# A decoder layer on one core: scores issued ahead of the state-space stages, S5 result and GELU by halves, and two moves before the MLP

## The reference, cut to what matters

```python
proj = _modulate(_rmsnorm(h, norm_mix), sh1, sc1) @ w_in           # u, q, k, v, qi, ki, wi
y = S5(u)                                                          # 32 groups x 64 states
y = jax.nn.gelu(y); y_ssm = y * jax.nn.sigmoid(y @ w_glu + b_glu)
s_idx = sum_h(relu(qi_h @ ki) * wi_h); sel = top_k(s_idx, 128)     # causal
p = softmax(where(selected, q @ k / 8, -inf)); y_attn = p @ v      # 8 heads
h = h + g1 * (concat(_rmsnorm(y_ssm), _rmsnorm(y_attn)) @ w_out)
up = _causal_dwconv(_modulate(_rmsnorm(h, norm_ffn), sh2, sc2) @ w_up, conv_w, conv_b)
h = h + g2 * ((jax.nn.gelu(gate) * val) @ w_down)
```

## Time and profile before

| | |
|---|---|
| median of 3 runs | 800.43 us (797.33 to 802.19) |
| profiled execution | 801.28 us |
| its span | 799.5 us |
| mean granted TensorE clock | 0.951 |
| busy: TensorE, VectorE, ScalarE, GpSimd | 89%, 61%, 41%, 32% |

### The profile page before, as it was taken

One profiled execution on the slowest core, in us unless ns is written; L12 is line 12 of the kernel. 1 busy time (PEld: TensorE's weight loads), 2 busy tenths in 40 slices (PEclk: granted clock), 3 DMA queues, 4 the chain that ended last, 5 costly groups with the idle time before them and its releaser, 6 DMA issues.

```text
span 799.5 us, 9833 instructions
## 1 busy us (share of the span) xinstructions
PE 709.3 (89%) x3524; PEld 565.6 (71%) x3524; DVE 488.4 (61%) x872; ACT 328.2 (41%) x476; POOL 257.6 (32%) x204
## 2 busy tenths in 40 slices
PE   0689999998668858889949999999999999999998
PEld 0667876776555635668849788888887887888886
DVE  2989588997599977868852576566545554100005
ACT  4246345346321452523246544544555555210110
POOL 1006697308501300000220444334442444334440
PEclk9999999999588869999979999999999999999999
DMA  9932131260033583753370322333223222332212
GB/s 338 341 109 80 53 106 53 79 184 1 1 45 46 106 315 109 264 211 106 105 260 31 106 69 89 105 105 105 70 88 105 97 67 99 106 105 101 64 46 106
DMA packets 65608, 91.46 MB, mean 114 GB/s; under 512 B 11914, under 2 KB 39330, under 8 KB 65443
## 3 DMA queue, kind: packets, MB, share of 16 engines
q1 hardware_dynamic: 60800, 84.72, 33.7%
q10 hardware_dynamic: 4771, 6.26, 2.3%
HBM read 86.28 MB, written 4.69 MB: 114 GB/s over the span
## 4 chain that ended last, share of the span: by engine, by line
PE 72%; DVE 17%; ACT 4%; issue 3%; DMA 3%; ACTq 1%; SPq 0%; DVEq 0%
PE bank L1544 21%; PE bank L1546 20%; PE bank L1545 20%; PE bank L1549 3%; DVE arena L1102 2%; PE bank L1857 2%; PE bank L1770 1%; PE bank L1750 1%; DVE w_lo L1096 1%; DMA y_dram<-xh 1%; DVE arena L1248 1%; DMA xh<-in_x 1%; DVE stat L1049 1%; DVE stat L1245 1%; PE bank L1880 1%
## 5 line engine op out<-in xcount | busy, mean ns | idle before, releaser
L466 POOL TENSOR_TENSOR w_lo<-w_raw,w_hi 128x2048 fp32r<-128x2048 f32 x35 | 161.5, 4614 | 408.0 <-ACT w_hi L658 199.4
L1544 PE MATMUL bank<-act_hi,w_hi 128*128 128x512 f32 (+2 forms) x384 | 148.5, 387 | 9.9 <-DVE act_lo L1480 8.4
L1545 PE MATMUL bank<-act_lo,w_hi 128*128 128x512 f32 (+2 forms) x384 | 147.4, 384 | 0.0
L1546 PE MATMUL bank<-act_hi,w_lo 128*128 128x512 f32 (+2 forms) x384 | 147.3, 384 | 0.0
L1544 PE MATMUL bank<-w_hi,act_hi 128*128 128x512 f32 x240 | 100.7, 420 | 5.8 <-DVE act_lo L1137 4.2
L1546 PE MATMUL bank<-w_hi,act_lo 128*128 128x512 f32 x240 | 96.8, 403 | 0.0
L1545 PE MATMUL bank<-w_lo,act_hi 128*128 128x512 f32 x240 | 96.7, 403 | 0.0
L1544 PEld LDWEIGHTS bank<-act_hi,w_hi 128*128 128x128 f32 x384 | 73.4, 191 | 25.2 <-issue 9.0
L658 ACT ACTIVATE w_hi<-w_raw 128x2048 fp32r<-128x2048 f32 x26 | 49.8, 1914 | 100.4 <-PE bank L1546 85.8
L1545 PEld LDWEIGHTS bank<-act_lo,w_hi 128*128 128x128 f32 x384 | 73.3, 191 | 14.7 <-issue 0.2
L1546 PEld LDWEIGHTS bank<-act_hi,w_lo 128*128 128x128 f32 x384 | 73.3, 191 | 14.6
(11 more groups left out here) (296 smaller groups left out, 1180.5 us busy)
## 6 DMA issues: line engine op xcount, KB each, us to landing
w_raw<-in_w_up SPq DMA_DIRECT2D x44, 512.0 KB, 4.4
w_raw<-in_w_down SPq DMA_DIRECT2D x22, 512.0 KB, 4.2
w_raw<-in_w_in SPq DMA_DIRECT2D x10, 1024.0 KB, 5.1
arena<-in_w_ada SPq DMA_DIRECT2D x4, 2048.0 KB, 18.6
arena<-in_w_ada SPq DMA_DIRECT2D x8, 1024.0 KB, 8.3
xh<-in_x SPq DMA_DIRECT2D x8, 512.0 KB, 8.0
w_raw<-in_w_out SPq DMA_DIRECT2D x4, 1024.0 KB, 12.9
s_mem<-in_w_ada SPq DMA_DIRECT2D x4, 1024.0 KB, 8.5
```

What stands on the lines that cost most here:

```text
L466: nc.gpsimd.tensor_tensor(w_lo[:, slot, 0:width], w_raw[:, slot, 0:width], w_hi[:, slot, 0:width].bitcast(F32), ALU.subtract).then_inc(S[" ...
L1544: T.matmul(dst, lhs_hi, rhs_hi, start=start, stop=False)
L1545: T.matmul(dst, lhs_hi, rhs_lo, start=False, stop=False)
L1546: return T.matmul(dst, lhs_lo, rhs_hi, start=False, stop=stop)
```

## The change

Four edits. In TensorE's list the S5 stages of a unit come one pass later, after the scores of the next pair and directly ahead of the unit's own probabilities. The store and load of y and the GELU are done by halves of the channels, at units 20 and 23, and the gate stages of S5 move: `g` of the first half from unit 22 to 21, the four `glu` from 25 to 28 to 26 to 29, with the squares of y accordingly. The loads of the second gate leave ScalarE's queue and stand in SP's, behind the first two units of the MLP. The low part of `U_UP` is VectorE's instead of GpSimd's.

```diff
-         15: ("y", 0, 0), 18: ("y", 1, 0), 22: ("g", 0, 0), 24: ("g", 1, 0),
-         25: ("glu", 0, 0), 26: ("glu", 1, 0), 27: ("glu", 2, 0), 28: ("glu", 3, 0)}
+         15: ("y", 0, 0), 18: ("y", 1, 0), 21: ("g", 0, 0), 24: ("g", 1, 0),
+         26: ("glu", 0, 0), 27: ("glu", 1, 0), 28: ("glu", 2, 0), 29: ("glu", 3, 0)}
+GELU_AT = {20: 0, 23: 1}
-SQUARE_AT = {19: (0,), 20: (1,), 28: (2, 4), 29: (5,), 30: (6,), 31: (7,)}
+SQUARE_AT = {19: (0,), 20: (1,), 28: (2,), 29: (4,), 30: (5,), 31: (6, 7)}
@@ SP
+            def y_load(half):
+                ns = slice(256 * half, 256 * half + 256)
+                sp.wait_ge(S[f"y_stored{half}"], 16)
+                load(y_ssm[:, :, ns], y_dram.rearrange("(a p) n -> p a n", p=P)[:, :, ns], f"y_loaded{half}")
+
+            sp.wait_ge(S["s5_state"], 2)
             sp.wait_ge(S["y_mm"], 2)
             later_ada(0, (0,))
+            y_load(0)
             sp.wait_ge(S["y_mm"], 4)
             later_ada(0, (1,))
-            sp.wait_ge(S["y_stored"], 16)
-            load(y_ssm, y_dram.rearrange("(a p) n -> p a n", p=P), "y_loaded")
+            y_load(1)
@@ SP
-            with sp.Fori(0, UPS) as j:
+            def up_units(j):
...
+            up_units(0)
+            sp.wait_ge(S["ada_used"], 6)
+            for i in range(2):
+                load(gate2_w[i], wa[:, :, 5120 + 512 * i:5632 + 512 * i], f"ada_next_loaded{i}")
+            load(gate2_row, b_ada[0, 5120:6144].partition_broadcast(P), "gate2_row")
+            with sp.Fori(1, UPS) as j:
+                up_units(j)
@@ GpSimd
-            pool.wait_ge(S["lo_ready"], U_UP)
-            for n in (U_UP, U_UP + 1):
-                pool.wait_ge(S["hi_ready"], n + 1)
-                lo(slot(n))
+            pool.wait_ge(S["lo_ready"], U_UP + 1)
+            pool.wait_ge(S["hi_ready"], U_UP + 2)
+            lo(slot(U_UP + 1))
@@ ScalarE
-                if stage == "y" and half:
-                    act.wait_ge(S["y_read"], 4)
-                    act.dma_start(y_dram.rearrange("(c i) n -> c (i n)", i=CHUNK), chunk_rows).then_inc(S["y_stored"], 16)
+                if stage == "y":
+                    ns = slice(256 * half, 256 * half + 256)
+                    act.wait_ge(S["y_read"], 2 * half + 2)
+                    act.dma_start(y_dram.rearrange("(c i) n -> c i n", i=CHUNK)[:, :, ns], chunk_in[:, :, ns]
+                                  ).then_inc(S[f"y_stored{half}"], 16)
@@ ScalarE
-                if i == 21:
-                    act.wait_ge(S["y_loaded"], 16)
-                    for a in range(TT):
-                        nc.scalar.activation(y_ssm[:, a, :], y_ssm[:, a, :], ACT.Gelu_apprx_tanh).then_inc(S["gelu_ready"], 1)
+                if i in GELU_AT:
+                    half = GELU_AT[i]
+                    ns = slice(256 * half, 256 * half + 256)
+                    act.wait_ge(S[f"y_loaded{half}"], 16)
+                    nc.scalar.activation(y_ssm[:, :, ns], y_ssm[:, :, ns], ACT.Gelu_apprx_tanh).then_inc(S["gelu_ready"], 1)
@@ ScalarE
-            act.wait_ge(S["ada_used"], 6)
-            for i in range(2):
-                act.dma_start(gate2_w[i], w_ada[0].rearrange("(p k) n -> p k n", k=KD)[:, :, 5120 + 512 * i:5632 + 512 * i]
-                              ).then_inc(S[f"ada_next_loaded{i}"], 16)
-            act.dma_start(gate2_row, b_ada[0, 5120:6144].partition_broadcast(P)).then_inc(S["gate2_row"], 16)
@@ VectorE
             late_ada(5)
+            lo(U_UP)
@@ TensorE
-                    pe.wait_ge(S["gelu_ready"], TT)
+                    pe.wait_ge(S["gelu_ready"], half + 1)
@@ TensorE
                 for j in (i - 2, i - 1):
+                    if j in S5_AT:
+                        s5(*S5_AT[j])
                     if 0 <= j < ATT_UNITS:
                         turn_probs(j)
                     if 0 <= j - 1 < ATT_UNITS:
                         values(j - 1)
-                for j in (i, i + 1):
-                    if j in S5_AT:
-                        s5(*S5_AT[j])
```

More of the change, by code:

```diff
@@ L289, in layer @@
             "zeros_stored", "m_loaded", "zero_ready", "lag_d_added", "u_t", "u_t_read", "state_mm",
-            "state_read", "s5_state", "y_mm", "y_read", "y_stored", "y_loaded", "gelu_ready", "g_t",
+            "state_read", "s5_state", "y_mm", "y_read", "y_stored0", "y_stored1", "y_loaded0", "y_loaded1", "gelu_ready", "g_t",
             "g_t_read", "glu_in", "glu_mm", "tanh_z", "glu_read", "ss_y_ready", "yn_ready", "mix_t",
```

## The result

The changed kernel takes 795.09 us (median of 17 runs, 791.91 to 797.05), the kernel before 799.33 (17 runs, 797.33 to 802.56). The ratio is 0.9943, interval 0.993 to 0.9957: 4.2 us less for 17 runs of each, 0.6%, inside the range of 780 to 799 but within the 1% that the prediction called no change. It had said 789.5, 11 us less than before. The profiled execution has a span of 793.3 us (799.5) and a mean granted clock of 0.958 (0.951).

The account below looks back on a forecast made before the run. Bound before the MLP by VectorE in the pair loop, then ScalarE's queue; from 443 us by TensorE. 1.5 + 5.0 + 4.5 + 0.2 = 11.2 us off 801.28 gave 790.1, for the median 789.5; range 780 to 799.

Parts of the forecast that it names:

- Loads of the second gate: Before the MLP: with the loads off ScalarE's queue, all behind comes 4.5 us earlier; bounds 4.0 and 4.6.
- Low part: U_UP's low part on VectorE, at the second residuals: 0.2 us gained; bounds 1.4 lost, 1.6 gained.
- Entry: Pair loop's start: TensorE stands 4.7 us, clock falls, yet the scan comes 1.5 us earlier; bounds 4 earlier, 3 later.
- Table loads: Split GELU adds two ScalarE table loads of 1.28 us, 2.6 us together, half of it on the next pair's exponentials.
- From the scan to 292.5 VectorE is full, so the 1.5 us pass through.: Scan to top-k's end: VectorE has no idle time, so the entry's 1.5 us gain arrives whole.
- slower: Rival: y of half two starts late behind VectorE's evictions, gate products come a pair later; 809 us, chance 0.07.
- After top-k 5.0: Top-k's end to the norm: waits shrink, 6.3 us by the sum, 5.0 taken after table loads; bounds 0 and 10.8.
- up to the last gate product: From pair 26 TensorE sets the end: four products 16.1, four units 5.4, scores 1.1, together 22.6 us.
- if the four products run at the low clock for a few us: Lower bound of the term after top-k: in this case nothing of the 5.0 us is gained.
- the start eats it: Rival: standing and low clock put the S5 chain 3 us late, loop ends within 1 us of before; 796, chance 0.22.
- All waits go: Rival: scan 4 us earlier and the 10.8 us of waits after top-k vanish; 781 us, chance 0.13.
- What the prediction named as its refutation: Scan later than 218, second GELU waiting over 3 us beyond top-k's end, or modulation still 4 us after the square.

Follow-up runs that it names:

- values in their old place: Changed kernel with the value projections of units 0 and 1 back ahead of the scores of units 2 and 3; 793.77 us, ratio 0.9922.
- The run with y moved: Changed kernel with y of half two placed behind the values of unit 15 and ahead of the probabilities of unit 17; 794.21 us, ratio 0.994.
- the kernel with the other two places mended: Changed kernel with value projections ahead of unit 2's scores and y of half two behind unit 15's values, gate products left at 26 to 29; 790.72 us.
- the three places: Changed kernel with value projections ahead of unit 2's scores, y of half two behind unit 15's values, gate products at 25 to 28; 783.04 us.

## Why the prediction was wrong, by its own steps

**Right.** *Loads of the second gate*: 4.5 forecast, 4.7 measured alone, the one term of the sum that is shown. *Low part*: 0.2 forecast, 0.2 measured, which is not told from nothing, and no operation above 3 us at the residuals. *Entry*: TensorE stood 4.69 us for the eviction (4.7 forecast), the clock fell, pair 4 was evicted at 197.34 (197 to 200 forecast, and 15.6 us behind unit 0, where the forecast had 13.8 to 16.8), the scan came 2.1 us earlier against unit 0 (1.5 forecast, chosen between bounds of 4 earlier and 3 later, so in part luck). *Table loads*: 1.28 us each, and the GELU starts 1.30 us behind the load's start (282.53 to 283.83) and 1.29 the second time. The Trainium skill (ScalarE: Activation LUTs, What ACT_TABLE_LOAD costs) counts a drain of 1.38 us more per load; these rows, like the earlier trace rows, have no room for it, so the forecast's choice of the trace held and the loss lies elsewhere.

**Wrong, first step: "From the scan to 292.5 VectorE is full, so the 1.5 us pass through."** It was full because its scores were ready, and the change itself took that away. The new order puts y of half two behind the scores of unit 20, which need VectorE's eviction of unit 18, and ahead of the scores of unit 22. Then 9.4 us of y, ScalarE's copies of it and the probabilities of units 18 and 19 stand between two evictions, and VectorE's own work between them is shorter by the wait: 2.24 us, then 1.56 for g. It is not the lead that is lost there. A VectorE 4.5 us earlier finds the same wait (2.13, values in their old place), and its lead passes. It is a new cost of the order, which the sum put at nothing. From the scan to the end of top-k were 76.3 us before (216.17 to 292.50) and are 80.6 now (212.61 to 293.17); 1.2 of this is g's low part, which lies in it now, so 3.0 us are lost in this stretch. Counted from unit 0, top-k ends at 111.5 us instead of 109.3. The run with y moved gives 2.3 of them back. I had costed the wait for y only in the "slower" rival, as a long wait of the GELU, and not at the scores that stand behind y.

**Wrong, second step: "After top-k 5.0".** The sum had 38.3 us from top-k's end to the norm, 42.7 were measured (293.17 to 335.91), so that of the 5.0 us 1.9 came (45.85 - 42.74, less the 1.2 us of g's low part that moved into top-k). TensorE's part "up to the last gate product", 22.6, was taken with all products at 4.03 us. It was 25.9: from 302.56 to 324.46 + 4.0. In it 2.3 us are the first product at 1.2 GHz (7.58 against 5.30) and 1.6 the scores ahead of it (2.72 against 1.13); without them it would be 22.0, so the sum was otherwise 0.6 too long. Behind the last product the tail took 7.4 instead of 6.2 us, with ScalarE's squares last (2.89). I had written this clock down as a bound, "if the four products run at the low clock for a few us", but took the stand ahead of unit 28 for nothing. The kernel before had this cost already. Its first gate product, and what follows it:

```profile
303.39 1.09 PE L1797 MATMUL bank<-arena,ones 1*128 1x512 f32 x2 [2.22 <-issue]
...
308.75 1.29 PE L1750 MATMUL bank<-arena 64*128 64x512 f32 x4
```

TensorE stood 2.22 us ahead of it, and the product took 5.36 us, not 4.03, with the clock at 0.50 from 306 to 309. In the change, products one unit later leave TensorE nothing to do while VectorE evicts pair 26. What the clock alone costs at this place is measured by rows, not by a run that removes it: with TensorE kept busy there the first product was short again, and pair 24 to the norm stayed at 42.7. That the place of the products costs 6 us is shown for the kernel with the other two places mended; in the changed kernel it is about 1 us, not told from nothing.

**The rivals.** The time is that of "the start eats it" (796, chance 0.22), and the loop did end 1.0 us earlier against unit 0, as it said. Its mechanism was wrong, so its number is luck: the scan was not late but early, and the gain was lost behind it at two other places. The 783 us of the three places lie near the 781 of "All waits go", but that is another kernel and says nothing for this rival.

**What the prediction named as its refutation** (a scan after 218, a long wait of the second GELU, a late modulation) did not happen, and it was still wrong. Two of its signs of being right did fail: top-k ended at 293.2 and not near 291, and the norm came at 335.9 and not near 332, in an execution that was 1.5 us early at unit 0. The list of refutations looked for failures of what the change touches, not for the next thing in line.

## What to carry to other kernels

When an edit reorders one engine's list, an engine that shows no waits in the profile before can get new ones. Before counting on such a stretch, write down for each of its inputs what that input stands behind in the new order: here y's products came to stand between two evictions of VectorE, which then waits 2.1 to 2.6 us however early it is. Work placed ahead of a wait covers it and, at the entry of this loop, kept TensorE's clock; moved behind the wait it cost both, 2.4 + 2.1 us at the scan. Where mended places sit one behind the other, test them together: alone they brought 0 to 2 us, none told from noise, and together 10 more than the change.

## What the runs showed of the hardware

- TensorE was given 1.2 GHz behind the stands of 4.69, 2.73 and 1.98 us in the changed kernel and of 1.90 us ahead of unit 28 in the kernel with two places, and 3.71 us of turnings of an identity in the stand of 4.69 us kept it at 2.4 GHz. At the entry the filling ended 1.05 us before the wait did. Ahead of unit 28 it ran at the low clock, ended after the wait would have, made the scores 2.2 us later, and the norm came no earlier.
- A small operation of VectorE stretched as long as GpSimd's low part beside it. In the changed kernel, VectorE's step of the reciprocal root and GpSimd's operation at the same time:

```profile
405.21 4.51 DVE L1061 SCALAR_TENSOR_TENSOR stat<-stat 128x1 f32<-128x1 f32 x1
409.75 0.16 DVE L1062 SCALAR_TENSOR_TENSOR stat<-stat 128x1 f32<-128x1 f32 x1
```

The next step, with GpSimd done, takes 0.16 us, as this one does elsewhere, and the operation of GpSimd at 405.11 takes 4.59. It was there before as well (4.43 us at 412.36); no edit of this change meets it. The low part for which TensorE stands 1.98 us at 411.23 comes right behind these steps.
